# Two attention stages of a fused model on one core: probabilities times values as one plain fp32 product in place of two split ones

## The reference, cut to what matters

```python
# _nsa, "sparse": 6 query heads of 64, 2 key/value heads
p_c = masked_softmax(q @ k_cmp);  o_c = p_c @ v_cmp     # 31 compressed keys
p_s = masked_softmax(q @ k_sel);  o_s = p_s @ v_sel     # selected blocks
p_w = masked_softmax(q @ k_win);  o_w = p_w @ v_win     # window of 512
y_b = (gate0 * o_c + gate1 * o_s + gate2 * o_w) * silu(n_z)
# _dilated_mixer: 3 groups (dilation 1, 4, 16), 2 heads of 64 in each
p, m, den = masked_softmax(q @ k);  o = p @ v
y_c = softmax_over_groups(m + log(den)) * o * silu(d_z)
h = h + concat(y_a, y_b, y_c) @ w_out
```

## Time and profile before

| | us |
|---|---|
| median of the runs | 1399.73 |
| span of the profiled execution, first to last instruction | 1397.3 |
| PE busy, share of the span | 1321.2 (95%) |
| PE weight loads busy | 1094.2 (78%) |
| DVE busy | 794.2 (57%) |
| ACT busy | 531.6 (38%) |
| POOL busy | 29.0 (2%) |
| PE on the chain that ended last | 82% of the span |
| DVE and ACT on it | 11% and 4% |

### The profile page before, as it was taken

The page is one execution under the profiler, slowest core; times in us unless marked ns, Lnnn a source line. Parts: engine busy times, 40 slices in busy tenths (PEclk is TensorE's granted clock), DMA queues, the critical chain, the costliest instruction groups (busy, mean ns, idle before and its releaser), DMA issues.

```text
span 1397.3 us, 16364 instructions
## 1 busy us (share of the span) xinstructions
PE 1321.2 (95%) x6203; PEld 1094.2 (78%) x6203; DVE 794.2 (57%) x1112; ACT 531.6 (38%) x753; POOL 29.0 (2%) x32
## 2 busy tenths in 40 slices
PE   7899999999999888899999999999999899977997
PEld 6688888888877777788888888888887787765876
DVE  6744445444458775564544444455685578876554
ACT  5522233233334544433322232343233445555334
POOL 5000000000000000000000000000000000020000
PEclk9999999999999999999999999999999999988999
DMA  5222322222331100222232222325342110102321
GB/s 180 91 95 93 112 90 90 84 92 84 101 99 51 55 31 31 87 94 91 90 107 95 99 75 83 102 83 155 121 151 62 59 52 25 61 0 105 114 68 61
DMA packets 120888, 119.43 MB, mean 85 GB/s; under 512 B 13500, under 2 KB 117896, under 8 KB 120584
## 3 DMA queue, kind: packets, MB, share of 16 engines
q1 hardware_dynamic: 120784, 118.76, 26.4%
q10 hardware_dynamic: 56, 0.01, 0.0%
HBM read 114.57 MB, written 4.19 MB: 85 GB/s over the span
## 4 chain that ended last, share of the span: by engine, by line
PE 82%; DVE 11%; ACT 4%; issue 2%; DMA 1%; SPq 0%; DVEq 0%; ACTq 0%
PE psum L1743 25%; PE psum L1744 25%; PE psum L1745 25%; DVE w_lo L1089 2%; PE psum L2096 1%; ACT w_hi L628 1%; PE psum L2082 1%; PE psum L2068 1%; DVE xg_lo L1319 1%; DMA band<-in_c_band 1%; PE psum L1783 1%; PE psum L2172 0%; PE psum L2154 0%; DVE du L1420 0%; PE psum L2190 0%
## 5 line engine op out<-in xcount | busy, mean ns | idle before, releaser
L1743 PE MATMUL psum<-xg_hi,w_hi 128*128 128x512 f32 x1072 | 426.9, 398 | 3.9 <-DVE xg_lo L1657 2.9
L1745 PE MATMUL psum<-xg_hi,w_lo 128*128 128x512 f32 x1072 | 418.1, 390 | 0.0
L1744 PE MATMUL psum<-xg_lo,w_hi 128*128 128x512 f32 x1072 | 418.0, 390 | 0.0
L1743 PEld LDWEIGHTS psum<-xg_hi,w_hi 128*128 128x128 f32 x1072 | 201.9, 188 | 47.9 <-DVE xg_lo L1657 3.5
L1745 PEld LDWEIGHTS psum<-xg_hi,w_lo 128*128 128x128 f32 x1072 | 201.5, 188 | 42.6
L1744 PEld LDWEIGHTS psum<-xg_lo,w_hi 128*128 128x128 f32 x1072 | 201.9, 188 | 40.6 <-issue 1.4
L1206 DVE TENSOR_TENSOR w_lo<-w_raw,w_hi 128x2048 fp32r<-128x2048 f32 x42 | 96.3, 2292 | 152.6 <-ACT w_hi L707 152.6
L1230 DVE TENSOR_TENSOR w_lo<-w_raw,w_hi 128x2048 fp32r<-128x2048 f32 x32 | 73.4, 2293 | 115.9 <-ACT w_hi L726 115.9
L1743 PE MATMUL psum<-act_hi,w_hi 128*128 128x512 f32 x352 | 137.2, 390 | 0.0
L1744 PE MATMUL psum<-act_lo,w_hi 128*128 128x512 f32 x352 | 137.0, 389 | 0.0
L1745 PE MATMUL psum<-act_hi,w_lo 128*128 128x512 f32 x352 | 136.9, 389 | 0.0
(11 more groups left out here) (375 smaller groups left out, 1735.2 us busy)
## 6 DMA issues: line engine op xcount, KB each, us to landing
w_raw<-in_ffn_w_gate SPq DMA_DIRECT2D x22, 1024.0 KB, 5.0
w_raw<-in_ffn_w_up SPq DMA_DIRECT2D x22, 1024.0 KB, 5.0
w_raw<-in_w_in SPq DMA_DIRECT2D x16, 1024.0 KB, 5.5
w_raw<-in_ffn_w_down SPq DMA_DIRECT2D x16, 768.0 KB, 4.8
w_raw<-in_ffn_w_down SPq DMA_DIRECT2D x16, 640.0 KB, 4.5
w_raw<-in_mla_w_o SPq DMA_DIRECT2D x4, 1024.0 KB, 5.1
w_raw<-in_w_out SPq DMA_DIRECT2D x4, 1024.0 KB, 5.5
w_raw<-in_w_ple_gate SPq DMA_DIRECT2D x4, 1024.0 KB, 5.0
```

What stands on the lines that cost most here:

```text
L1743: pe.matmul(o, wh, xh, start=start, stop=False, skip_group_check=True)
L1744: pe.matmul(o, wh, xl, start=False, stop=False, skip_group_check=True)
L1745: return pe.matmul(o, wl, xh, start=False, stop=stop, skip_group_check=True)
```

## The change

- **Values in plain fp32.** V and the transposed probabilities stay fp32 and are no longer split. One fp32 matmul with 64 weight columns takes the place of each pair, in both mixers. Its result has 64 partitions, so two heads share bank 7: even heads write partitions 0 to 63, odd ones 64 to 127. DVE's subtractions for `pn_lo`, `ptc_lo`, `xg_lo`, `v_st` and `vc_st` go, and so do ACT's copies of the upper halves and DVE's additions.
- **Gating in pairs.** `sparse_out` multiplies the gate by a whole bank once per pair of heads, at indices 21 and 37 of the loop and in the dilated stage.
- **Work begun in the sparse loop.** The dilated V is transposed at indices 30, 34 and 38 into the bank that `project` has just left, and copied by ACT at 31, 35 and 39. The scores of dilated steps 0 and 1 stand at indices 48 and 49. In the dilated stage scores then run two steps ahead.
- **Dilated values.** Head 0's three groups use bank 7 one after the other, with a copy by DVE (`first_out`) between them and a fill of transposes of step 4 ahead of the second and the third. Head 1's use banks 7, 4 and 2, and all but the last column block are multiplied before the last step's probabilities are there.
- **Memory.** `k_st` now lies where the residual was, so its copies wait until that has been stored (`x_stored`); SP issues the store one weight load earlier. The keys of dilated head 1 are in `xg_hi` and `xg_lo`.

The diff, cut to its core:

```diff
@@ sparse values (PE)
-                    o, u, g = bank[7], s // NB, h // 3
-                    pe.wait_ge(sem("n_lo"), s + 1)
+                    o, u, g = bank[7][64 * (h % 2):64 * (h % 2) + 64, :], s // NB, h // 3
+                    pe.wait_ge(sem("n_kept"), s + 1)
                     if s % 8 == 0:
-                        pe.wait_ge(*(sem("n_sum"), h) if h else (sem("c_lo"), 2))
+                        pe.wait_ge(sem("c_kept"), 2)
+                        if h >= 2:
+                            pe.wait_ge(sem("n_sum"), h // 2)
                         r = slice(h % 3 * 32, h % 3 * 32 + 32)
-                        for part, pt in enumerate((ptc_hi, ptc_lo)):
-                            pe.matmul(o[:, :], vc_st[r, g, :], pt[r, g, :], start=part == 0, stop=False, skip_group_check=True)
-                    for part, pt in enumerate((pn_hi, pn_lo)):
-                        mm = pe.matmul(o[:, i * P:T], v_st[:, b, g, i, :], pn_row(pt, u, i), start=False, stop=s % 8 == 7 and part == 1,
-                                       skip_group_check=True)
-                    mm.then_inc(sem("n_pv"), 1)
+                        pe.matmul(o[:, :], vc_tok[r, g, :], ptc[r, g, :], start=True, stop=False, skip_group_check=True)
+                    pe.matmul(o[:, i * P:T], v_tok[:, b, g, i, :], pn_row(pn, u, i), start=False, stop=s % 8 == 7,
+                              skip_group_check=True).then_inc(sem("n_pv"), 1)
@@ sparse transposes (PE)
-                        pe.wait_ge(sem("n_lo"), s - 1)
+                        pe.wait_ge(sem("n_kept"), s - 1)
@@ sparse loop (PE)
+                    if s in (30, 34, 38):
+                        dilated_values((30, 34, 38).index(s))
+                    if s in (48, 49):
+                        dilated_scores(s - 48)
@@ sparse loop (DVE)
-                        add_halves(r, bank[7], br[r, h // 2, :], sem("n_sum"), root, sq_sum)
-                    if 0 <= s - 4 < len(NSTEP):
-                        turned_lo(s - 4)
+                    if s in (21, 37):
+                        sparse_out(s // 16 - 1)
+            def sparse_out(pair):
+                dve.wait_ge(sem("n_pv"), 16 * pair + 16)
+                dve.tensor_tensor(br[:, pair, :], br[:, pair, :], bank[7][:, :], ALU.mult).then_inc(sem("n_sum"), 1)
@@ dilated values (PE)
+                def first_values(g):
+                    pe.wait_ge(sem("dv_kept"), 3)
+                    pe.wait_ge(sem("d_kept"), first_fill(4))
+                    n = D_ORDER[0].index(g)
+                    if n == 0:
+                        pe.wait_ge(sem("n_sum"), 3)
+                    else:
+                        pe.wait_ge(sem("d_out"), n)
+                    for kb in (3, 2, 1, 0):
+                        mm = value(0, g, kb, kb, last_query(g, kb), kb == NB - 1, kb == 0)
+                    mm.then_inc(sem("d_pv"), 1)
+                def second_values():
+                    pe.wait_ge(sem("d_exp"), 7)
+                    pe.wait_ge(sem("d_kept"), first_fill(7))
...
+                    pe.wait_ge(sem("d_kept"), first_fill(8))
+                    for g in D_ORDER[1]:
+                        value(1, g, 0, 0, 0, False, True).then_inc(sem("d_pv"), 1)
+                for x in range(len(DSTEP)):
+                    if x + 2 < len(DSTEP):
+                        dilated_scores(x + 2)
+                    if x == 4:
+                        first_values(D_ORDER[0][0])
+                        pe.wait_ge(sem("d_probs"), x + 1)
+                        for n in range(3):
+                            turn_fill(x, n)
+                            if n < 2:
+                                first_values(D_ORDER[0][n + 1])
+                    else:
+                        turn(x)
+                second_values()
@@ dilated (ACT), in this order
+                softmax_exp(0)
+                act.wait_ge(sem("u_done"), NT)
+                keys_hi(1, 0)
+                softmax_exp(1)
+                keys_hi(1, 1)
+                turned(0)
+                softmax_exp(2)
+                keys_hi(1, 2)
+                turned(1)
...
+                turned(4)
+                act.wait_ge(sem("n_sum"), 3)
+                softmax_exp(6)
+                y_hi(2)
+                turned(5)
+                softmax_exp(7)
+                y_hi(3)
+                turned(6)
@@ residual store (SP)
-                if n == n_mix + 8:
+                if n == n_mix + 7:
```

More of the change, by code:

```diff
@@ L180, in program @@
         mix_mem = ExitStack()
[L183 to L185 removed]
+        pn = sb("pn", [P, NB, (NB + 1) * P], stack=mix_mem)
+        k_st = sb("k_st", [P, 4, 2, T], F32R, mix_mem)
+        d_pt = sb("d_pt", [P, 8, T], stack=mix_mem)
         q_st = sb("q_st", [P, 6, T], F32R, mix_mem)
[L187 to L188 removed]
+        v_tok = sb("v_tok", [P, 2, 2, NB, 64], stack=mix_mem)
+        dv_tok = sb("dv_tok", [P, 3, NB, P], stack=mix_mem)
         br = sb("br", [P, 8, T], stack=mix_mem)
@@ L496, in d_keys, with d_value_bank @@
                 return k_st[:, n, 0, :], k_st[:, n, 1, :]
-            return tuple(x[:, :, :].rearrange("p a t -> p (a t)")[:, g * T:(g + 1) * T] for x in (pn_hi, pn_lo))
+            return xg_hi[:, 5 + g, :], xg_lo[:, 5 + g, :]
+        def d_value_bank(g):
+            return u_bank(KINDS.index("dv") + g)
         @block.sync
@@ L960, in nsa @@
                         keys_hi(0, g)
+                    if s in (31, 35, 39):
+                        dilated_values((31, 35, 39).index(s))
+                dilated_query(5)
             def dilated():
@@ new lines, in dilated @@
+                act.wait_ge(sem("u_done"), NT)
[6 more added lines that the diff above has]
+                turned(1)
+                softmax_exp(3)
+                act.wait_ge(sem("conv_step"), 14)
+                y_hi(0)
+                turned(2)
+                softmax_exp(4)
+                turned(3)
+                y_hi(1)
+                softmax_exp(5)
@@ L1023, in dilated @@
-                out(3)
-                for f in (0, 1):
-                    y_hi(f)
-                gate(0)
-                act.wait_ge(sem("n_sum"), 6)
-                out(4)
-                for f in (2, 3):
-                    y_hi(f)
-                gate(1)
-                gate(2)
-                out(5)
+                    if g == 0:
+                        turned(7)
                 y_hi(4)
                 for f in (5, 6, 7):
-                    act.wait_ge(sem("d_gated"), (2, 1, 3)[f - 5])
+                    act.wait_ge(sem("d_gated"), f - 4)
@@ L1576, in normalise @@
                        .then_inc(sem("n_probs"), 1)
-                def turned_lo(s):
-                    i, u = NSTEP[s][2], s // NB
-                    dve.wait_ge(sem("n_hi"), s + 1)
-                    dve.tensor_tensor(pn_cells(pn_lo, u, i), bank[5 + s % 2][:, 0:(i + 1) * P].rearrange("p (j q) -> p j q", q=P),
-                                      pn_cells(pn_hi, u, i).bitcast(F32), ALU.subtract).then_inc(sem("n_lo"), 1)
-                for s in range(len(NSTEP) + 7):
+                for s in range(len(NSTEP) + 1):
                     if s < len(NSTEP):
@@ L2160, in scores, with dilated, turn_fill @@
                     mm.then_inc(sem("d_scored"), 1)
+            def dilated():
+                def turn_fill(x, n):
+                    f = first_fill(x) + n
+                    if f >= 2:
+                        pe.wait_ge(sem("d_kept"), f - 1)
+                    for m, b in enumerate(D_FILLS[DSTEP[x][1]][n]):
+                        mm = pe.transpose(bank[5 + f % 2][:, m * P:(m + 1) * P], d_probs(x)[:, b * P:(b + 1) * P], ident[:, :])
+                    mm.then_inc(sem("d_turned"), 1)
@@ L2196, in dilated @@
-                scores(0)
-                pe.wait_ge(sem("n_lo"), len(NSTEP))
-                def turn_values(g):
-                    for j in range(NB):
-                        mm = pe.transpose(bank[5 + g][:, j * P:(j + 1) * P], du[:, 6 + g, j * P:(j + 1) * P], ident[:, :])
-                    mm.then_inc(sem("dv_turned"), 1)
-                turn_values(0)
-                turn_values(1)
-                pe.wait_ge(sem("n_sum"), 6)
-                turn_values(2)
-                for x in range(len(DSTEP) + 1):
-                    if x + 1 < len(DSTEP):
-                        scores(x + 1)
-                    if x == 1:
-                        pe.wait_ge(sem("dv_lo"), 2)
-                    if x == 5:
-                        values(0)
-                    if x >= 1:
-                        turn(x - 1)
@@ L2217, in dilated, with value @@
-                values(1)
+                    if x == 0:
+                        pe.wait_ge(sem("n_kept"), len(NSTEP))
+                    for n in range(len(D_FILLS[DSTEP[x][1]])):
+                        turn_fill(x, n)
+                def value(j, g, kb, first, last, start, stop):
+                    c = d_cell(g, kb, first)
```

(3 more changed lines are left out.)

258 lines of the change are left out of this document (95 added, 163 removed).

## The result

The changed kernel took 1406.09 us in the median of six runs, the kernel before 1399.95 in six beside them: a ratio of 1.0045, with a 95% interval of 1.0031 to 1.0059. That is 0.45% slower; the forecast was +9.9 us, the measurement says +6.1 (6.3 by the ratio). The slowdown is clear of noise, but it is smaller than the 7 us from which the prediction calls a kernel slower: 1406.09 lies under its bound of 1406.7, in "the same" (0.29), and not in "slower" (0.59).

The account below looks back on a forecast made before the run. PE bounds the sparse loop; the dilated stage is a chain from engine to engine. Terms +24.7, +1.2, -7.8 and -8.2 sum to +9.9 us: 1409.6 us, range 1403 to 1415, with A and C 1393 to 1417.

Parts of the forecast that it names:

- slower: Whole kernel: measured above 1406.7 us, chance 0.59.
- the same: Whole kernel: measured between 1392.7 and 1406.7 us, within about 0.5% (7 us) of no change, chance 0.29.
- values of the loop: Sparse loop on PE: fp32 value products and changes of tile take 43.5 us instead of 18.8, +24.7 us.
- transposes of the dilated V: Sparse loop: twelve transposes now stand there in three groups of 0.4 us, +1.2 us.
- waits for `pn_lo`, `ptc_lo`: Sparse loop: PE's waits for these DVE results go, 7.0 us at heads' ends and 0.8 for ptc_lo, -7.8 us.
- dilated stage: Step 43's values to w_out: 48.2 us against 56.4, -8.2; scores 4 at 17.0, done 24.2, second values 39.2.
- The drain: Value products on PE: changing to 64 columns and back drains TensorE, so every visit pays, 0.36 us.
- rival A: Narrow tile costs nothing to enter or leave: 14.6 us go in the loop, about 1.5 in the stage, 1393.5; chance 0.22.
- visit: PE entering and leaving the 64-column tile for value products: 0.36 us each, seven visits a head in the sparse loop.
- Rival D: Sparse loop: stalls at the heads have another cause, so 7.0 us stay, 1416.6; chance 0.12 together with C.
- rival C: Long fp32 phases run at the lower clock, or a wait returns at the pairs: +5.7, 1415; chance 0.12 with D.
- rival B: Dilated stage shortens far more, w_out starting at 40 us: sum +1.7, 1401; chance 0.10.

Follow-up runs that it names:

- lo_first: The kernel before, with DVE's subtraction that makes pn_lo moved ahead of the two additions closing a head: 1393.35 us, ratio 0.9954.
- wide_sparse: The changed kernel, with sparse-loop value products using all 128 weight columns, V padded with zeros: 1395.52 us, ratio 0.9966.
- paired: The changed kernel, with sparse values issued two steps at a time, so PE enters the 64-column tile four times a head, not seven: 1398.89 us, ratio 0.9996.
- low_back: The changed kernel, with the dilated stage's 18 DVE subtractions put back, PE waiting for them, their results unused: 1414.59 us, ratio 1.0114.
- scores_late: The changed kernel, with the first two dilated score steps back behind the sparse loop's last values: 1406.70 us, ratio 1.0048.

## Why the prediction was right, step by step

The forecast was +9.9 us, "slower" with 0.59, and a range of 1393 to 1417; the measurement is +6.1 in medians. From step 43's values backward and forward the changed trace gives +15.7 for the loop (144.5 against 128.8 from the first score) and -9.3 for the stage: +6.4. Term by term:

| term | forecast | measured | by |
|---|---|---|---|
| values of the loop | +24.7 | +23.3 | stretches from the last projection product to the mask: 66.7 against 43.2, less the transposes' 1.2; and 1.1 behind the last mask |
| transposes of the dilated V | +1.2 | +1.2 | heads with them: 24.90 and 24.51 against 24.12 |
| waits for `pn_lo`, `ptc_lo` | -7.8 | -8.8 | stretches from a mask to the next last projection product: 73.1 against 81.9 |
| dilated stage | -8.2 | -9.3 | same boundaries in both traces |
| sum | +9.9 | +6.4 | |

The three terms that miss do so to the same side: values 1.4 too dear, waits 1.0 and stage 1.1 too small a gain, together 3.5.

**Values of the loop.** The term that was mis-sized most. A head takes 19.95 us in `lo_first`, between the starts of its compressed products, and 24.12 in the changed kernel: +4.17, where the forecast had +4.51. The steps show what of it is streaming and what the tile: from the last projection product's start to the mask's, in us,

| columns of the values | before | wide_sparse | changed | forecast for the change |
|---|---|---|---|---|
| 512 compressed, then 128 and 256 | 1.72 | 2.29 | 2.39 | +0.70 |
| 384 | 1.04 | 1.34 | 1.68 | +0.66 |
| 512 | 1.04 | 1.44 | 1.78 | +0.76 |
| 128 | 0.68 | 0.68 | 1.03 | +0.41 |
| 256 | 0.64 | 0.83 | 1.18 | +0.56 |

Columns one to two are the fp32 passes, two to three the tile: 0.34 or 0.35 wherever a step is visited alone, and 0.10 in a head's first step, where the rows of the tile change anyway, as forecast (0.36 + 0.15 - 0.41). The fp32 passes cost what 4 passes say, but for 128 columns nothing: the split pair that went was itself slower than its columns. I had priced it at 0.17, the distance from its first start to the scores behind it, and left out that these are held up too: their pair of 256 columns then takes 0.29 up to the mask and not 0.23. In `lo_first`, where such a pair and one of 256 follow each other, both take 0.28 or 0.29, whatever their columns:

```profile
1137.30 0.33 PE L2098 MATMUL psum<-pn_hi,v_st 128*128 128x128 f32 x1
1137.47 0.28 PE L2098 MATMUL psum<-pn_lo,v_st 128*128 128x128 f32 x1
1137.58 0.33 PE L2098 MATMUL psum<-pn_hi,v_st 128*128 128x256 f32 x1
1137.75 0.28 PE L2098 MATMUL psum<-pn_lo,v_st 128*128 128x256 f32 x1
1137.87 0.33 PE L2070 MATMUL psum<-k_st,q_st 128*128 128x128 f32 x2
```

Altogether 4.3 a head by the steps. The 0.15 between that and +4.17 is the rest of the stall that `lo_first` still has at each head's end: without it a head of the old products would take 19.80, by this count.

**The drain** was the step on which the sign hung (rival A, 0.22). It is confirmed from three sides: its size in the changed trace (0.34 for 0.36), its disappearance with the tile's width (wide_sparse), and its proportion to the visits and not the products (paired). By the prediction's own totals the sign turns at a visit of 0.14 us (9.9 of the 16.1 us have to go), not at the 0.12 that it names; nothing hangs on it. With it gone the kernel would have been 0.34% faster than before, near the 1393.5 of the rival: 1395.5.

**The waits.** Right in place, and 1.0 us too small. What went at the five heads' ends is 7.8 us, the wait for `ptc_lo` 0.9. The first is more than the 7.0 of the listed stalls, since PE lost 0.15 at each beyond what the list counts. Rival D (they stay) falls by the list of PE's waits above. But the forecast took them for a benefit of the new precision; most of it, 6.8 us, was one of the order of DVE's list, to be had alone.

**The dilated stage.** The intermediate times were forecast at 17.0, 24.2, 39.2 and 48.2 and came at 18.1, 25.6, 39.6 and 47.1. POOL releases scores 4 as said. The second values took 7.5 us at a clock of 0.79, where I had 7.8, with 1.7 for the clock. That they agree is partly luck: in three of the six traces with these products the clock was 1.00 there and they took 6.0. The last hand-overs were cheaper. How much of the 9.3 us is the clock of the stage, 0.86 where it was 0.79, no run here separates. The first values ran at clock 1.00, so rival C fell, and 47.1 is far from rival B's 40. The prediction put the gain on DVE's subtractions "mostly" and "the rest" on the two early score steps. The first is shown by low_back in sign and order of size. The second is borne out by the trace of scores_late, with 1.7 us up to the second values, but the runs can't tell it from nothing. The 0.36 that the prediction takes for a visit here is hardly on the path: a whole tile saves 0.3 us for four visits.

**The span.** That the profiled span rose by 10.1, so near to 9.9, speaks less for the forecast than it seems: 3.6 us of it are scatter ahead of the loop, and they cover that the loop was forecast 2.4 too long and the stage 1.1 too short a gain.

## What to carry to other kernels

In the loop, where PE never waits, a matmul that uses half of the array's columns between matmuls that use them all cost a third of a us each time, however short it was: pad its weights to the full width, with zeros where the other half is read, or issue several such products together. In the stage where PE waits for others, the same padding was worth only 0.3 us. A change of precision that removes work from an idle engine and adds passes to the full one lost here in the loop that TensorE bounds and won in the stage that is a chain through several engines; look at each stage by itself and keep only the half that pays. And before an algorithm is changed to get rid of a wait, see whether the instruction that PE waits for stands behind one that nobody waits for.

## What the runs showed that I had not expected

The visit's price doesn't depend on the length of the value product: 0.35 for 128 columns, 0.34 for 512, though the long one would have given the next load 0.86 us to hide in. A plain fp32 product of 128 columns takes no longer in its place than the split pair of fp32r products (0.68 us for the step in both), whereas at 512 columns it takes 0.40 more. And one moved line in DVE's order was worth 6.6 us, about as much as the whole change costs. The same 30 value products before `w_out` took 7.5 us in three executions and 6.0 in three others, at a granted clock of 0.79 and 1.00.
